# Attention, retention and gated-MLP blocks on one core: where head 0's values, modulation's loads and modulation's turning stand

## The chip, the cores and the metric

One core of one Trainium2 chip. The metric is the device time of one launch in microseconds, the median of the runs of a kernel. TensorE (PE) multiplies into PSUM, VectorE (DVE) and ScalarE (ACT) read PSUM and prepare operands, GpSimd (POOL) and SyncE (SP) issue the loads, POOL computes a few small powers too.

## The reference

Everything is float32 on 256 tokens of width 2048. The change touches the first layer, grouped-query attention with a gate, and the product that modulates the second block:

```python
proj = h @ w_in                                   # 2048 x 5120
q, k, v, g = jnp.split(proj, [...], axis=-1)      # 16 query heads, 4 key heads of 128
q = apply_rope(rms_norm(q, q_gain), cos, sin) * (A_HEAD_DIM ** -0.5)
k = apply_rope(rms_norm(k, k_gain), cos, sin)
s = jnp.einsum('bkgqd,bskd->bkgqs', qb, k)
p = jax.nn.softmax(s, axis=-1)
o = jnp.einsum('bkgqs,bskd->bkgqd', p, v)
return (o * jax.nn.silu(g)) @ w_out
...
x = layer_norm(ALPHA * x + y, ln_gain[i], ln_bias[i])
...
mod = silu(c) @ w_mod + b_mod                     # 2048 x 12288, for the second block
```

Behind it come a retention layer with eight heads, a second block of window and indexed attention, and a gated MLP.

## The kernel before

**Products in three passes.** A product of float32 matrices is made of three matmuls: rounded weights times rounded activations, weight rest times rounded activations, rounded weights times activation rest (`product`, L420 to L422). So each weight chunk is loaded (`raw`), rounded by ACT into `w_hi` (`round_hi`, L401) and its rest is made by VectorE into `w_lo` (`split_lo`, L406). Weights come in blocks of four chunks of 4 x 128 rows; SP loads a chunk of the next block, in two halves, when TensorE has finished the chunk that held the buffer (`load`, L366).

**Attention.** The four key heads are called heads 0 to 3 here, each with its four query heads. For head i TensorE runs `pe_attention`: a block for the queries (512 columns, block 4i - 1), a block for key and value (256 columns, block 4i), a block for the gate (512 columns, block 4i + 1) and, for i > 0, a block of the output projection of the head before (block 4i + 2). Head 0 has blocks 0 to 2. So head 1 has blocks 3, 4, 5 and 6, head 2 blocks 7 to 10. Between the gate's chunks stand the turning of the normed queries and keys (L559, `turn_qk`) and the scores (L659). Between the output's chunks stand, as `between(c)`, the turning of the probabilities (L669) and the values (L677). Head 0 has no output block: its `between` steps run back to back after its gate block, with 19 filler matmuls of `pe_fill` (L565) in them. Heads 1 to 3 are one hardware loop.

**Who waits for whom.** VectorE in `vec_attention` makes `w_lo` chunk by chunk, norms and rotates the queries (L1157 to L1168, with a power on POOL, L1586) and later the key, splits the turned head output into `a_oh` and `a_ol` (L1248), and multiplies the values by the gate into `a_og` (L1231). In between it adds up modulation's product, `mod_pair`, eight steps of 1 MB of `w_mod` per head (L1075, L1081). The sum of a head is turned by TensorE (`pe_mod`, L571) after chunk 1 of the next head's second block, and VectorE reads it (`mod_read`, L1090). The query turning waits for `a_ol` of the head before. After head 0 VectorE computes the retention layer's decay constants (`vec_decay`, L1424 to L1454, some 40 tiny operations), and ACT scales z by ALPHA (L1013).

**POOL's queue** is in order: for heads 1 to 3 two modulation loads (L1571), the power of the query norm, two loads, the power of the key norm, four loads. Each load waits until VectorE has used up the buffer.

```python
with g.Fori(1, A_KV) as i:
    loads(i, 0, 2)
    a_power(i, 0)
    loads(i, 2, 4)
    a_power(i, 1)
    loads(i, 4, 8)
```

## Time and profile before

| | |
|---|---|
| median of 3 runs | 2299.97 us (2297.93 to 2300.0) |
| the profiled execution, its own time | 2298.13 us |
| its span | 2296.4 us |
| TensorE busy | 2242.6 us, 98% of the span |
| VectorE busy | 1681.7 us, 73% |
| ScalarE busy | 994.6 us, 43% |
| mean granted clock of TensorE | 0.996 of full |

Busy time on TensorE is time with a matmul in flight. A timeline row gives the start and the time to the end of the last instruction in it, in us from the span's start; an entry in brackets is idle time of the engine ahead of the row and what ended it. The granted clock is a share of 2.4 GHz: 1.00 is that level, 0.50 the lower one of 1.2 GHz. The profiled execution's own time is 1.7 us above its span and 1.8 us below the median of the runs.

### The profile page before, as it was taken

The numbers are of one execution on the slowest core, as the hardware profiler recorded it, in microseconds if no ns is written. First come the engines' busy times: TensorE is split into PE (matmuls) and PEld (weight loads), VectorE is DVE, ScalarE is ACT, GpSimd is POOL, SyncE is SP. The second block draws the span as 40 slices with busy tenths as digits, with TensorE's granted clock in tenths as the row PEclk, the third lists the DMA queues.
The fourth block names the chain that finished last, engine by engine and source line by source line (L and its number), as shares of the span: only waits on it lengthen the run. The fifth ranks groups of instructions, "written<-read, shape, count | busy, mean of one in ns | idle before, by whom it ended". The sixth has DMA issues, their size and how long they took to land.

```text
span 2296.4 us, 28927 instructions
## 1 busy us (share of the span) xinstructions
PE 2242.6 (98%) x10724; PEld 1851.6 (81%) x10724; DVE 1681.7 (73%) x1871; ACT 994.6 (43%) x1017; POOL 141.6 (6%) x202
## 2 busy tenths in 40 slices
PE   7999999999999999999999999999999999999998
PEld 6888888888878888788787778777888888888886
DVE  5788877988877778677795676985655666665567
ACT  4543433534434434343443456454444344444434
POOL 2110010010000000000011001000000000000000
PEclk9999999999999999999999999999999999999999
DMA  7877775687777777777746546455555555555553
GB/s 256 287 262 258 262 257 202 203 327 274 269 263 274 261 255 274 257 269 270 244 167 202 187 138 166 145 166 183 184 184 194 188 183 189 192 186 183 192 190 131
DMA packets 260288, 503.57 MB, mean 219 GB/s; under 512 B 14705, under 2 KB 68385, under 8 KB 259328
## 3 DMA queue, kind: packets, MB, share of 16 engines
q1 hardware_dynamic: 228480, 381.73, 49.9%
q0 software_dynamic: 31376, 119.80, 15.1%
q10 hardware_dynamic: 368, 1.18, 0.1%
q8 instruction: 41, 0.67, 0.1%
q14 instruction: 23, 0.19, 0.0%
HBM read 498.90 MB, written 3.69 MB: 219 GB/s over the span
## 4 chain that ended last, share of the span: by engine, by line
PE 85%; DVE 6%; DMA 4%; issue 2%; ACT 2%; SPq 0%; POOL 0%; DVEq 0%; POOLq 0%; ACTq 0%
PE pair_t L420 26%; PE pair_t L422 25%; PE pair_t L421 25%; DMA raw<-in_attn_w_in_dram 2%; PE turn L559 2%; DVE w_lo L406 1%; ACT w_hi L401 1%; PE sc L827 1%; PE sc L819 1%; DVE m_acc L1081 1%; PE sc L1678 1%; PE sc L677 1%; PE sc L659 0%; PE turn L1687 0%; DMA raw<-in_w_down_dram 0%
## 5 line engine op out<-in xcount | busy, mean ns | idle before, releaser
L406 DVE TENSOR_TENSOR w_lo<-raw,w_hi 128x2048 fp32r<-128x2048 f32 (+1 forms) x364 | 815.8, 2243 | 486.6 <-ACT w_hi L401 482.2
L401 ACT ACTIVATE w_hi<-raw 128x2048 fp32r<-128x2048 f32 (+1 forms) x367 | 689.0, 1879 | 1037.5 <-DMA raw<-in_ret_w_in_dram 340.9
L420 PE MATMUL pair_t<-w_hi,x_hi 128*128 128x512 f32 (+1 forms) x2080 | 814.3, 392 | 15.1 <-DVE w_lo L406 9.2
L422 PE MATMUL pair_t<-w_hi,x_lo 128*128 128x512 f32 (+1 forms) x2080 | 799.4, 384 | 0.0
L421 PE MATMUL pair_t<-w_lo,x_hi 128*128 128x512 f32 (+1 forms) x2080 | 798.8, 384 | 0.0
L420 PEld LDWEIGHTS pair_t<-w_hi,x_hi 128*128 128x128 f32 x2080 | 393.1, 189 | 101.2 <-DVE w_lo L406 11.9
L422 PEld LDWEIGHTS pair_t<-w_hi,x_lo 128*128 128x128 f32 x2080 | 392.8, 189 | 78.0
L421 PEld LDWEIGHTS pair_t<-w_lo,x_hi 128*128 128x128 f32 x2080 | 393.4, 189 | 72.9 <-issue 0.2
L1081 DVE SCALAR_TENSOR_TENSOR m_acc<-m_raw,csilu,m_acc 128x1024 f32<-128x1024 f32 x180 | 230.8, 1282 | 7.0 <-DMA m_raw<-in_w_mod_dram 3.5
L420 PE MATMUL pair_t<-w_hi,f_hh 128*128 128x512 f32 x352 | 138.2, 393 | 1.8 <-DVE f_y L2261 0.8
L421 PE MATMUL pair_t<-w_lo,f_hh 128*128 128x512 f32 x352 | 137.0, 389 | 0.0
L422 PE MATMUL pair_t<-w_hi,f_hl 128*128 128x512 f32 x352 | 137.0, 389 | 0.0
L1571 POOL DMA_DIRECT2D m_raw<-in_w_mod_dram x96 | 68.9, 718 | 936.0 <-DVE m_acc L1081 921.3
L420 PE MATMUL pair_t<-w_hi,r_oh 128*128 128x512 f32 x256 | 102.8, 401 | 0.1
L422 PE MATMUL pair_t<-w_hi,r_ol 128*128 128x512 f32 x256 | 99.7, 390 | 0.0
L421 PE MATMUL pair_t<-w_lo,r_oh 128*128 128x512 f32 x256 | 99.6, 389 | 0.0
L420 PEld LDWEIGHTS pair_t<-w_hi,f_hh 128*128 128x128 f32 x352 | 66.1, 188 | 16.3 <-DVE f_y L2261 1.8
L422 PEld LDWEIGHTS pair_t<-w_hi,f_hl 128*128 128x128 f32 x352 | 66.1, 188 | 13.8
L421 PEld LDWEIGHTS pair_t<-w_lo,f_hh 128*128 128x128 f32 x352 | 66.1, 188 | 13.3
L1241 DVE TENSOR_TENSOR z<-z,pair_t 128x512 f32<-128x512 f32 x88 | 56.3, 681 | 14.5 <-PE pair_t L422 14.2
L2657 POOL TENSOR_TENSOR rstd<-var,minus_half 128x1 f32<-128x1 f32 x6 | 4.3, 711 | 870.9 <-DVE var L2250 870.9
L420 PEld LDWEIGHTS pair_t<-w_hi,r_oh 128*128 128x128 f32 x256 | 48.1, 188 | 12.0 <-issue 1.7
(362 smaller groups left out, 2145.1 us busy)
## 6 DMA issues: line engine op xcount, KB each, us to landing
m_raw<-in_w_mod_dram POOLq DMA_DIRECT2D x96, 1024.0 KB, 6.1
raw<-in_ret_w_in_dram SPq DMA_DIRECT2D x192, 512.0 KB, 4.6
raw<-in_w_up_dram SPq DMA_DIRECT2D x176, 512.0 KB, 4.2
raw<-in_w_down_dram SPq DMA_DIRECT2D x88, 512.0 KB, 4.6
raw<-in_attn_w_in_dram SPq DMA_DIRECT2D x64, 512.0 KB, 4.6
raw<-in_ret_w_out_dram SPq DMA_DIRECT2D x64, 512.0 KB, 4.8
raw<-in_w_in_dram SPq DMA_DIRECT2D x56, 512.0 KB, 4.5
raw<-in_attn_w_out_dram SPq DMA_DIRECT2D x32, 512.0 KB, 5.1
```

Source lines behind the costliest of these rows:

```text
L401: act.activation(chunk(w_hi, c, width), chunk(raw, c, width), ACT.Copy).then_inc(sem("hi"), 1)
L406: v.tensor_tensor(chunk(w_lo, c, width), chunk(raw, c, width), chunk(w_hi, c, width).bitcast(F32), ALU.subtract).then_inc(sem("lo"), 1)
L420: pe.matmul(to, xh, wh, start=start, stop=False)
L421: pe.matmul(to, xh, wl, start=False, stop=False)
L422: return pe.matmul(to, xl, wh, start=False, stop=stop)
L559: mm = pe.transpose(to[:, i * P:(i + 1) * P], src[:, t, m * P:(m + 1) * P], ident[:, :])
L677: mm = pe.matmul(sc[t][:, h * A_HD:(h + 1) * A_HD], a_pT[:, h % 2, k, t * P:(t + 1) * P], a_v[:, k, :], start=k == 0, stop=k == NT - 1)
L819: mm = pe.matmul(sc[0][:, s * T:(s + 1) * T], r_kT[:, k, s * P:(s + 1) * P], r_qT[:, k, :], start=k == 0, stop=k == 1)
L827: mm = pe.matmul(sc[t][:, :], r_s[:, s, t * P:(t + 1) * P], r_v[:, s, :], start=s == 0, stop=s == NT - 1)
L1081: ins = v.scalar_tensor_tensor(out=m_acc[:, :], in0=w, scalar=cc, in1=m_acc[:, :], op0=ALU.mult, op1=ALU.add)
L1241: ins = v.tensor_tensor(z[:, t, c * CB:(c + 1) * CB], z[:, t, c * CB:(c + 1) * CB], pair[order[c]][t][:, :], ALU.add)
L1571: g.dma_start(m_raw[:, u % 2, :, :], w_m[:, 2 * u:2 * u + 2, bass.ds(2 * step * CB, 2 * CB)])\
```

## The change

Head 1 is taken out of the hardware loop and written out; the loops run over heads 2 and 3. In it,

- TensorE's `between` steps of head 0 (turning the probabilities, values) stand after chunks 0, 1 and 2 of head 1's first block, and the fillers are gone;
- the turning of modulation's sum stands after chunk 3 of head 1's second block, not after chunk 1, and the turning of head 0's output `a_og` behind it, not before the block;
- VectorE splits that output (`vec_a_turn`) behind the key's norm, not behind the query's;
- chunk 3 of head 1's first block is rounded and split at the end of head 0, behind the last copy of turned probabilities;
- the decay constants are computed at the end of head 1, not of head 0, on VectorE and ACT;
- ACT scales the two halves of z between its roundings in head 1.

And for heads 1 to 3, POOL's first two modulation loads stand behind the query norm's power.

TensorE, the end of head 0 before, with the turnings of probabilities (a_p) and the values (a_v):

```order
L659 MATMUL sc<-a_kT,a_qT 128x256 x4
L669 MATMUL turn<-ident,a_p 128x128 x8
L565 MATMUL pair_t<-ident 128x128 x19
L677 MATMUL sc<-a_v,a_pT 128x128 x4
L669 MATMUL turn<-ident,a_p 128x128 x4
```

The same place in the changed kernel, followed by the end of head 1's second block (128x256), modulation's turning (m_acc) and the output's (a_og); "..." stands for the projection's matmuls:

```order
L660 MATMUL sc<-a_kT,a_qT 128x256 x4
L420 MATMUL pair_t<-w_hi,x_hi 128x512
...
L670 MATMUL turn<-ident,a_p 128x128 x8
...
L678 MATMUL sc<-a_v,a_pT 128x128 x4
...
L678 MATMUL sc<-a_v,a_pT 128x128 x8
...
L422 MATMUL pair_t<-w_hi,x_lo 128x256
L571 MATMUL sc<-ident,m_acc 128x128 x8
L559 MATMUL turn<-ident,a_og 128x128 x8
```

A wide chunk of head 1 now stands ahead of each piece of head 0, and both turnings stand behind the narrow block.

VectorE in head 1 of the changed kernel, from the query's last scaling to the split of the turned output (a_ol); before, the row of a_ol stood right behind the first `w_lo` row:

```order
L1186 TENSOR_TENSOR a_q<-a_q,a_rs 128x512 x2
L406 TENSOR_TENSOR w_lo<-raw,w_hi 128x4x256
L406 TENSOR_TENSOR w_lo<-raw,w_hi 128x2048
L1106 TENSOR_REDUCE modc<-sc 128x4 x2
...
L1186 TENSOR_TENSOR a_k<-a_k,a_rs 128x128 x2
L1270 TENSOR_TENSOR a_ol<-turn,a_oh 128x512 x2
```

The split of the output has moved from ahead of modulation's reading to behind the key.

POOL in the loop over the heads, before:

```order
L1571 DMA m_raw<-in_w_mod_dram 128x2x1024
...
L1581 REGISTER_ALU
L1586 TENSOR_TENSOR a_rs<-a_ss,minus_half 128x8
L1570 REGISTER_ALU
```

and in the changed kernel:

```order
L1626 ISA
L1610 TENSOR_TENSOR a_rs<-a_ss,minus_half 128x8
L1594 ISA
L1595 ISA
L1595 DMA m_raw<-in_w_mod_dram 128x2x1024
```

The power now comes first in each trip, and the loads that stood ahead of it follow it.

The diff:

```diff
@@ -608,6 +608,7 @@
 
         def pe_attention(pe, i):
             first = isinstance(i, int) and i == 0
+            second = isinstance(i, int) and i == 1
 
             def arrived(c):
                 if first:
@@ -617,23 +618,23 @@
                     pe.wait_ge(sem("a_sum_z"), 2 + 4 * (i - 1) - 1)
 
             def mod(c):
-                if c == 1 and not first:
+                if c == (3 if second else 1) and not first:
                     pe_mod(pe, i - 1)
 
             def turn_x(c):
                 if c < 2:
                     pe_turn_x(pe, c + 2)
-            project(pe, a_block(i, 0), pair[0], before=arrived, after=turn_x if first else None, lead=first)
-            if first:
-                pe_params(pe)
-            else:
-                pe_a_turn(pe, i)
+
+            def attend_first(c):
+                if c < 3:
+                    between(c + 1, 0)
 
             def kv_free(c):
                 if c == 0 and not first:
                     pe.wait_ge(sem("a_krot"), i)
                     pe.wait_ge(sem("a_sum_z"), 2 + 4 * (i - 1))
-            project(pe, a_block(i, 1), pair[1], width=2 * A_HD, before=kv_free, after=mod)
+                if c == 1 and second:
+                    pe.wait_ge(sem("a_og"), 1)
 
             def q_read(c):
                 if c == 0:
@@ -660,7 +661,7 @@
                                    a_kT[:, :], start=True, stop=True)
                 mm.then_inc(sem("a_score"), 1)
 
-            def turn_probs(h):
+            def turn_probs(h, i):
                 pe.wait_ge(sem("a_prob"), 4 * i + h + 1)
                 if h >= 2:
                     pe.wait_ge(sem(f"a_pT{h % 2}"), 2 * i + 1)
@@ -670,7 +671,7 @@
                                           a_p[:, h, t, k * P:(k + 1) * P], ident[:, :])
                 mm.then_inc(sem("a_p_turned"), 1)
 
-            def values(h):
+            def values(h, i):
                 pe.wait_ge(sem(f"a_pT{h % 2}"), 2 * i + h // 2 + 1)
                 for t in range(NT):
                     for k in range(NT):
@@ -691,27 +692,31 @@
                     scores(2)
                     scores(3)
 
-            def between(c):
+            def between(c, i=i):
 
                 if c == 1:
-                    turn_probs(0)
-                    turn_probs(1)
+                    turn_probs(0, i)
+                    turn_probs(1, i)
                 elif c == 2:
                     pe.wait_ge(sem("a_prob"), 4 * i + 4)
-                    values(0)
-                    turn_probs(2)
-                    values(1)
-                    turn_probs(3)
+                    values(0, i)
+                    turn_probs(2, i)
+                    values(1, i)
+                    turn_probs(3, i)
                 elif c == 3:
-                    values(2)
-                    values(3)
+                    values(2, i)
+                    values(3, i)
+            project(pe, a_block(i, 0), pair[0], before=arrived,
+                    after=turn_x if first else attend_first if second else None, lead=first)
+            if first:
+                pe_params(pe)
+            elif not second:
+                pe_a_turn(pe, i)
+            project(pe, a_block(i, 1), pair[1], width=2 * A_HD, before=kv_free, after=mod)
+            if second:
+                pe_a_turn(pe, i)
             project(pe, a_block(i, 2), pair[0], before=q_read, after=along_gate)
-            if first:
-                for c in range(CH):
-                    between(c)
-                    if c == 1:
-                        pe_fill(pe, pair[1][0], 19)
-            else:
+            if not first:
                 pe_a_output(pe, i, between)
 
         def pe_turn_x(pe, q):
@@ -839,7 +844,8 @@
             pe_turn_x(pe, 0)
             pe_turn_x(pe, 1)
             pe_attention(pe, 0)
-            with pe.Fori(1, A_KV) as i:
+            pe_attention(pe, 1)
+            with pe.Fori(2, A_KV) as i:
                 pe_attention(pe, i)
             pe_fill(pe, turn[0], 15)
             pe_a_turn(pe, A_KV)
@@ -857,8 +863,10 @@
         def act_attention(act, i, n, rest):
 
             first = isinstance(i, int) and i == 0
+            second = isinstance(i, int) and i == 1
             H = lambda j, c: round_hi(act, a_block(i, j), c, 2 * A_HD if j == 1 else CB)
-            H(0, 3)
+            if not second:
+                H(0, 3)
             for c in range(2 if first else 3):
                 H(1, c)
             act.wait_ge(sem("products"), CH * a_block(i, 0) + 4)
@@ -866,13 +874,19 @@
                 act.activation(a_sq[:, t, :], pair[0][t][:, :], ACT.Square).then_inc(sem("a_square"), 1)
             if first:
                 H(1, 2)
-            if not first:
+            if first:
+                act_params(act)
+            elif not second:
                 act_a_turn(act, i)
-            else:
-                act_params(act)
             H(1, 3)
+            if second:
+                act.wait_ge(sem("turned"), KC // 2)
+                act.wait_ge(sem("turn_lo"), KC // 2)
+                act.activation(z[:, 0, :], z[:, 0, :], ACT.Copy, scale=ALPHA).then_inc(sem("home"), 1)
             H(2, 0)
             H(2, 1)
+            if second:
+                act.activation(z[:, 1, :], z[:, 1, :], ACT.Copy, scale=ALPHA).then_inc(sem("home"), 1)
             H(2, 2)
             act.wait_ge(sem("products"), CH * a_block(i, 1) + 4)
             if not first:
@@ -882,6 +896,8 @@
             act.wait_ge(sem("a_qrot"), i + 1)
             for t in range(NT):
                 act.activation(a_sq[:, t, 0:A_HD], pair[1][t][:, 0:A_HD], ACT.Square).then_inc(sem("a_square"), 1)
+            if second:
+                act_a_turn(act, i)
             H(2, 3)
             act.wait_ge(sem("a_qk_turned"), 3 * i + 1)
             act.activation(a_qT[:, 0:2, :], gview(turn[0][:, :], 2), ACT.Copy).then_inc(sem("a_qT_act"), 1)
@@ -918,6 +934,8 @@
             if rest:
                 rest[1](1)
             turned(2)
+            if first:
+                round_hi(act, n, 3)
             if rest:
                 rest[1](2)
 
@@ -1006,16 +1024,14 @@
                 round_hi(act, 0, c)
             turn_hi(act, 0, True, range(6, 8))
             act_attention(act, 0, a_block(1, 0), None)
+
+            def rest_of(i):
+                return [lambda c: round_hi(act, a_block(i, 3), c), lambda c: round_hi(act, a_block(i + 1, 0), c)]
+            act_attention(act, 1, a_block(1, 3), rest_of(1))
             act_decay(act)
-            act.wait_ge(sem("turned"), KC // 2)
-            act.wait_ge(sem("turn_lo"), KC // 2)
-            for t in range(NT):
-                act.activation(z[:, t, :], z[:, t, :], ACT.Copy, scale=ALPHA).then_inc(sem("home"), 1)
             act.wait_ge(sem("toep"), 16)
-            with act.Fori(1, A_KV) as i:
-                act_attention(act, i, a_block(i, 3),
-                              [lambda c: round_hi(act, a_block(i, 3), c),
-                               lambda c: round_hi(act, a_block(i + 1, 0), c)])
+            with act.Fori(2, A_KV) as i:
+                act_attention(act, i, a_block(i, 3), rest_of(i))
             act_a_turn(act, A_KV)
             round_hi(act, R_B0 - 1, 3)
             round_hi(act, R_B0, 0)
@@ -1138,8 +1154,10 @@
 
             def M():
                 mod_pair(v, *todo.pop(0))
+            second = isinstance(i, int) and i == 1
             S_ = lambda j, c: split_lo(v, a_block(i, j), c, 2 * A_HD if j == 1 else CB)
-            S_(0, 3)
+            if not second:
+                S_(0, 3)
             for c in range(2 if first else 3):
                 S_(1, c)
                 if not first and c < 2:
@@ -1172,7 +1190,7 @@
                     if first:
                         vec_params(v)
                     S_(1, 3)
-                    if not first:
+                    if not first and not second:
                         vec_a_turn(v, i)
                     for c in range(3):
                         S_(2, c)
@@ -1183,6 +1201,8 @@
                             mod_read(v, i - 1)
                         if first or c < 2:
                             M()
+            if second:
+                vec_a_turn(v, i)
             S_(2, 3)
             if not first:
                 M()
@@ -1215,9 +1235,11 @@
                         rest[1](c - 1)
                 if c in (1, 2):
                     turned(2 * c - 1)
+                if first and c == 2:
+                    split_lo(v, n, 3)
                 if c < 3:
                     M()
-                elif first:
+                elif second:
                     vec_decay(v)
             assert not todo
             v.wait_ge(sem("a_prob"), 4 * i + 4)
@@ -1485,12 +1507,14 @@
                 split_lo(v, 0, c)
             turn_lo(v, 0, groups=range(6, 8))
             vec_attention(v, 0, a_block(1, 0), None)
-            with v.Fori(1, A_KV) as i:
-                vs.enter(i, 1, VEC_A)
-                vec_attention(v, i, a_block(i, 3),
-                              [lambda c: split_lo(v, a_block(i, 3), c),
-                               lambda c: split_lo(v, a_block(i + 1, 0), c)])
-            vs.leave(A_KV - 1)
+
+            def rest_a(i):
+                return [lambda c: split_lo(v, a_block(i, 3), c), lambda c: split_lo(v, a_block(i + 1, 0), c)]
+            vec_attention(v, 1, a_block(1, 3), rest_a(1))
+            with v.Fori(2, A_KV) as i:
+                vs.enter(i, 2, VEC_A)
+                vec_attention(v, i, a_block(i, 3), rest_a(i))
+            vs.leave(A_KV - 2)
             vec_layer_end(v, "a", R_B0 - 1, A_KV, 1)
             split_half(v, R_B0, 1, 0)
             turn_lo(v, 1, par[:, 0:KC], par[:, KC:2 * KC], behind={
@@ -1600,9 +1624,8 @@
             get(rows[:, 0, :], broadcast_row(ln_gain, 0, D), "rows_in")
             get(rows[:, 1, :], broadcast_row(ln_bias, 0, D), "rows_in")
             with g.Fori(1, A_KV) as i:
-                loads(i, 0, 2)
                 a_power(i, 0)
-                loads(i, 2, 4)
+                loads(i, 0, 4)
                 a_power(i, 1)
                 loads(i, 4, 8)
```

## Rows read from the trace of the kernel before

**Rows 1.** The page, part 1: busy us, share of the span, instructions.

```profile
PE 2242.6 (98%) x10724; PEld 1851.6 (81%) x10724; DVE 1681.7 (73%) x1871; ACT 994.6 (43%) x1017; POOL 141.6 (6%) x202
```

**Rows 2.** PE timeline, head 0 into 1: start, us, instruction, [idle before <-releaser].

```profile
84.54 1.04 PE L669 MATMUL turn<-ident,a_p 128*128 128x128 f32 x8
85.42 4.41 PE L565 MATMUL pair_t<-ident 128*128 128x128 f32 x38
95.86 0.47 PE L420 MATMUL pair_t<-w_hi,x_hi 128*128 128x512 f32 x1
...
117.75 1.03 PE L559 MATMUL turn<-ident,a_og 128*128 128x128 f32 x8
```

**Rows 3.** DVE timeline, 106 to 149 (head 0's end and head 1).

```profile
106.89 2.16 DVE L1231 SCALAR_TENSOR_TENSOR a_og<-sc,a_rinv,a_sg 128x128 f32<-128x128 f32 x8
...
112.90 1.22 DVE L406 TENSOR_TENSOR w_lo<-raw,w_hi 128x1024 fp32r<-128x1024 f32 x1 [1.65 <-ACT w_hi L401]
...
120.21 1.22 DVE L406 TENSOR_TENSOR w_lo<-raw,w_hi 128x1024 fp32r<-128x1024 f32 x1
...
128.26 1.22 DVE L406 TENSOR_TENSOR w_lo<-raw,w_hi 128x1024 fp32r<-128x1024 f32 x1
129.40 1.28 DVE L1248 TENSOR_TENSOR a_ol<-turn,a_oh 128x512 fp32r<-128x512 f32 x2
...
135.01 1.28 DVE L1090 TENSOR_REDUCE modc<-sc 128x512 f32 x2
...
147.96 0.49 DVE L1168 TENSOR_TENSOR a_k<-a_k,a_rs 128x128 f32<-128x128 f32 x2
```

**Rows 4.** PE timeline, waits and query turnings (L559).

```profile
51.58 0.58 PE L420 MATMUL pair_t<-w_hi,x_hi 128*128 128x256 f32 x1 [4.29 <-DVE w_lo L406]
...
135.15 0.80 PE L420 MATMUL pair_t<-w_hi,x_hi 128*128 128x512 f32 x1 [2.48 <-DVE w_lo L406]
...
147.77 1.03 PE L559 MATMUL turn<-ident,a_q 128*128 128x128 f32 x8
...
226.54 0.50 PE L420 MATMUL pair_t<-w_hi,x_hi 128*128 128x512 f32 x1 [0.29 <-DVE w_lo L406]
...
237.85 1.04 PE L559 MATMUL turn<-ident,a_q 128*128 128x128 f32 x8
```

**Rows 5.** Busy us (x count) of PE, PEld, DVE, ACT, POOL; PEclk; DMA share; GB/s.

```profile
50.00:56.00 6.00, 4.42 (x20) 4.42 (x21) 5.09 (x4) 5.67 (x4) 0.00 (x0) 0.50 0.32 119
99.40:106.70 7.30, 7.30 (x34) 6.05 (x33) 6.20 (x39) 7.02 (x5) 1.81 (x3) 1.00 0.75 270
118.54:124.38 5.84, 5.84 (x51) 5.84 (x50) 5.74 (x10) 1.61 (x5) 2.19 (x2) 1.00 0.98 326
195.00:214.00 19.00, 19.00 (x93) 15.95 (x92) 9.93 (x8) 4.53 (x5) 1.43 (x2) 1.00 0.58 178
```

**Rows 6.** PE timeline, head 1's output block, values and turnings after chunk 2.

```profile
180.66 1.05 PE L677 MATMUL sc<-a_v,a_pT 128*128 128x128 f32 x8
...
183.24 0.48 PE L420 MATMUL pair_t<-w_hi,a_oh 128*128 128x512 f32 x1
```

**Rows 7.** Head 2: SP and POOL timelines, and us to landing of those two halves.

```profile
216.43 0.93 SPq L366 DMA_DIRECT2D raw<-in_attn_w_in_dram  x2
...
216.49 1.65 POOL L1586 TENSOR_TENSOR a_rs<-a_ss,minus_half 128x8 f32<-128x8 f32 x1 [4.80 <-DVE a_ss L1159]
...
DMA to landing us min/median/max: 4.5/4.9/5.2
```

**Rows 8.** The same in a retention head: halves behind a POOL load.

```profile
855.68 0.71 POOL L1571 DMA_DIRECT2D m_raw<-in_w_mod_dram  x1 [11.55 <-DVE m_acc L1081]
...
856.16 0.93 SPq L366 DMA_DIRECT2D raw<-in_ret_w_in_dram  x2
...
DMA to landing us min/median/max: 6.3/6.7/7.1
```

**Rows 9.** Landing of block 5's chunk 0 in head 1, behind POOL's load.

```profile
DMA to landing us min/median/max: 7.0/7.7/8.4
```

## Prediction

> **What bounds the kernel now.** I read the page's busy shares first: TensorE is busy for 98% of the span [rows 1], so a change pays only where it takes out one of the few stretches in which TensorE waits, fills or runs at a low clock. The second view is TensorE's timeline where the change cuts. Between the last scores of head 0 (84.54) and the first projection of head 1 (95.86) stand 11.32 us, of which 4.41 are filler matmuls [rows 2]; head 1's first block then takes 21.89 us for four chunks, 5.5 each, and ends at 117.75. The third is VectorE's timeline behind it [rows 3]: from 106.89 to 148.38 VectorE works nearly without a break, and what TensorE needs in head 1 comes out of that one sequence. The fourth are TensorE's waits on it [rows 4], with the granted clock and the busy time of four stretches [rows 5] and one piece of head 1 that prices the moved code [rows 6]. The last is how loads of the SP and POOL queues land when both are asked for at once [rows 7 to 9].
>
> **Head 0's values between head 1's chunks.** Chunk 0 of block 3 (head 1's first) can start when the scores and the gate's reader are done, at about 84.6; its split copies are ready, and that of chunk 3 is now made inside head 0. The work put between the chunks is 0.88 us for the first turning (84.54 to 85.42), 2.58 (180.66 to 183.24, the same code in head 1's output block) and for the last two values at most 2.0, since two such and two turnings make the 2.58 [rows 2, 6]: 5.4 us. Block 3 ends at 84.6 + 21.9 + 5.4 = 111.9 in place of 117.75, 5.9 earlier; the fillers and the waits around them are gone.
>
> **Does VectorE follow?** Its decay constants (99.4 to 106.7, [rows 5]) move out of the way. The head's output a_og now waits for the last values, one chunk before 111.9, so 106.4: it starts at 106.5 and takes 2.1. Chunk 0's split of block 4 to chunk 2's start is 120.21 - 112.90 = 7.3, so chunk 2 begins at 115.9; from there to the end of chunk 3's split are 129.48 - 120.21 = 9.3 us of square sums, rotation and scaling of the queries [rows 3], which ends at 125.2. TensorE, whose turnings now stand behind the block, runs three narrow chunks (two took 5.84, [rows 5]) in 8.8 us and is ready for chunk 3 at 120.7. **A new wait of 4.5 us** stands there. A wait of 4.29 us in head 0 was followed by a granted clock of 0.50 [rows 4, 5], the 1.2 GHz level: 20 narrow matmuls took 4.42 us, so 24 take 5.2 to 5.3 and not 2.9 to 3.0: 2.3 more. Block 4 ends at 130.5, modulation's turning 0.8 later at 131.3.
>
> VectorE then waits for that turning before it reads it (before, it stood behind chunk 1 and nobody waited). From the read (135.01) to the end of a_k (148.38) are 13.4 us, and the split of the turned output, 1.2 net, now comes behind a_k [rows 3]. So the query turning, which asks for that split, starts at 131.3 + 13.4 + 1.2 = 145.9; it was 147.77 [rows 4]. Only 1.9 us of the 5.9 are left. TensorE has been idle since 143.2 (131.3, 0.8 for the head's turning, two chunks), 2.7 us. Behind the wait of 2.48 at 135.15 the same two chunks took 12.6 us to the query turning, in head 2 11.3 [rows 4]: 1.3 us for the clock, and I charge that once more. **Head 1 gives 0.6 us.** Bounds: 4.2 if no clock is lost (1.9 + 2.3), and a loss of about 1 if the low clock lasts longer in both places.
>
> **Decay constants at head 1's end** cost nothing: VectorE is busy for 9.93 of the 19 us between 195 and 214 [rows 5], so 9.1 idle us cover 7.2. Without the cover the next a_og would be late for the turning at the end of the block. The scaling of z in ACT goes into ACT's waits for loads (ACT is busy for 4.53 of those 19 us, 1.61 of the 5.84 after 118.54, [rows 5]). Chunk 3's rounding and split in head 0 were due anyway and only come earlier. PE's extra code is unrolled; the trace shows no time for that.
>
> **Modulation's loads behind the query norm's power.** In head 1 they went ahead of the raw chunks of block 5 and held them (7.0 and 8.4 us to land, [rows 9]); there the change helps, but that wait was replaced above. In heads 2 and 3 it does something else. The power starts at 216.49 and takes 1.65 [rows 7]; its input comes 1.7 us earlier when no POOL load stands before chunk 2, so it ends at 216.5, and both 1 MB loads go out there. SP issues the two halves of block 9's chunk 0 (the gate projection of head 2) at 216.43 and 0.56 later, and they landed in 4.5 and 5.2 us with nothing beside them [rows 7]. A half issued 0.48 us behind a POOL load took 6.3 us, the next one 7.1 [rows 8]. In the changed kernel the second half is about 0.45 behind, so it lands at 217.0 + 6.3 = 223.3 and not 222.2. ACT and VectorE round and split it at once, TensorE already waits 0.29 us for it at 226.54 [rows 4], and VectorE's sequence up to a_k starts from it. **Heads 2 and 3 lose 1.1 us each.** Bounds: +0.7 gained (the half keeps its 4.5) to 3.2 lost (it takes 8.4, as in [rows 9]).
>
> The trace lets the queue that came first go first: the pair in [rows 9] waited for nearly the whole POOL load. The Trainium skill, "DMA: Bandwidth & Descriptors", section "Queues, rings and completion order", says that each DMA engine alternates between the queues at packet granularity. By that rule the 1 MB chunk and the 1 MB load would share from the start, the chunk would be 1 to 2 us late, and the worst bound could not occur; [rows 9] disagree, so I keep it.
>
> **Sum.** -0.6 + 2 x 1.1 = +1.6 us on the profiled execution's own time of 2298.13, so 2299.7. That execution lies 1.8 us below the median of the runs, 2299.97; on the median's scale the forecast is **2301.6 us**. About 0.2% (4.6 us) is what a measurement of this kernel can tell from no change, so I call this the same.
>
> **Rivals.**
> Faster: TensorE's clock stays up through both waits of head 1 (4.2 us) and the POOL loads come behind both raw halves, which land in 4.5 us (0.7 each): -5.6, 2294.4. For it: POOL's and SP's issues lie within 0.1 us of each other by my sum, and the landings in [rows 7] were free of any load. Against: the 4.29 and 2.48 us waits both did. It decides at a wait in head 1 below about 2 us. Chance 0.17.
> Slower: in heads 2 and 3 POOL's two loads get ahead of the whole chunk 0. Its second half lands like the 8.4 of [rows 9], 3.2 us late, and the wait of then some 3.5 us costs the clock (1.3): 4.5 x 2 - 0.6 = +8.4, 2308.4. It decides as soon as POOL issues before SP's first half at 216.43. For it: the two are even by my sum. Against: the power needs TensorE's last chunk, and SP needs only one chunk more. Chance 0.18.
> The loads' move does nothing in heads 2 and 3 because POOL issues behind both halves: -0.6, 2299.4. Chance 0.20.
> The forecast: 0.42. Something not named: 0.03.
>
> **Numbers.** Faster by over 0.2% is the first rival, 0.17. Slower by over 0.2% is the second with the upper edge of the forecast, 0.22. The same is 0.61. The range takes in the forecast and the third rival with their bounds and about half of each outer rival: 2295.0 to 2307.0.
>
> **What would show it.** Right: no fillers, block 3 done near 112; VectorE's chunk 3 of block 4 near 125 with TensorE waiting 4 to 5 us and a lowered granted clock; the query turning of head 1 near 146 behind a_ol; in heads 2 and 3 a wait of 1 to 2 us for chunk 0 of the third block. Wrong: a head 1 that keeps most of 5.9 us, or heads 2 and 3 that are no longer than before, or over 3 us longer each.

## The result and the profile after

The changed kernel took 2306.13 us in the median of eight runs (2303.46 to 2316.54), the kernel before, measured beside it, 2299.98 (2297.93 to 2304.02): ratio 1.0036, 95% interval [1.0021, 1.005] (the two medians alone give 1.0027). It is slower by 6 us; the forecast was +1.6 and no change that can be measured. Measured again later, with eleven runs, it gave 2303.42 and a ratio of 1.0023 [1.0009, 1.0038], 4.1 us above the median beside it. The profiled execution took 2303.46, 5.3 us more than that of before.

TensorE's share is a point lower, its idle time is up. Page, part 1:

```profile
span 2301.8 us, 28756 instructions
PE 2239.5 (97%) x10686; PEld 1849.7 (80%) x10686; DVE 1682.0 (73%) x1871; ACT 992.9 (43%) x1016; POOL 141.5 (6%) x202
```

TensorE's timeline where head 0's values now stand between head 1's chunks, and through head 1 (start, us, instruction, [idle before <-releaser]); it answers [rows 2, 4]:

```profile
84.95 0.50 PE L420 MATMUL pair_t<-w_hi,x_hi 128*128 128x512 f32 x1 [0.18 <-ACT a_sg L920]
...
119.87 0.38 PE L420 MATMUL pair_t<-w_hi,x_hi 128*128 128x256 f32 x1 [1.71 <-DVE w_lo L406]
...
127.83 0.58 PE L420 MATMUL pair_t<-w_hi,x_hi 128*128 128x256 f32 x1 [4.83 <-DVE w_lo L406]
...
132.24 1.04 PE L571 MATMUL sc<-ident,m_acc 128*128 128x128 f32 x8
133.11 1.04 PE L559 MATMUL turn<-ident,a_og 128*128 128x128 f32 x8
...
147.78 1.65 PE L559 MATMUL turn<-ident,a_q 128*128 128x128 f32 x8 [2.73 <-DVE a_ol L1270]
...
213.89 1.03 PE L559 MATMUL turn<-ident,a_og 128*128 128x128 f32 x8
...
235.95 0.50 PE L420 MATMUL pair_t<-w_hi,x_hi 128*128 128x512 f32 x1 [2.80 <-DVE w_lo L406]
...
307.55 1.03 PE L559 MATMUL turn<-ident,a_og 128*128 128x128 f32 x8
...
323.88 0.50 PE L420 MATMUL pair_t<-w_hi,x_hi 128*128 128x512 f32 x1 [2.92 <-DVE w_lo L406]
```

The fillers are gone and head 1's first projection starts at 84.95 in place of 95.86. The query turning of head 1 still starts at 147.78, where it was 147.77. Two waits before the chunks of block 4 and one before the query turning have eaten all of it. Two more waits of 2.80 and 2.92 us in heads 2 and 3 were 0.29 in head 2 before [rows 4].

VectorE over the same stretch (answers [rows 3]):

```profile
118.59 1.23 DVE L406 TENSOR_TENSOR w_lo<-raw,w_hi 128x1024 fp32r<-128x1024 f32 x1 [2.09 <-ACT w_hi L401]
...
126.55 3.42 DVE L406 TENSOR_TENSOR w_lo<-raw,w_hi 128x1024 fp32r<-128x1024 f32 x2
133.31 1.29 DVE L1106 TENSOR_REDUCE modc<-sc 128x4 f32<-128x512 f32 x2 [3.34 <-PE sc L571]
...
146.44 1.28 DVE L1270 TENSOR_TENSOR a_ol<-turn,a_oh 128x512 fp32r<-128x512 f32 x2
```

The split of chunk 2 waits for its rounded copy, and so for the second raw half; the norm and chunk 3's split come behind it, and then VectorE itself waits 3.34 us for TensorE's turning of modulation's sum. The granted clock in block 4's last chunk and behind the query turning, and VectorE in head 1's output block (answers [rows 5]: busy us of PE, PEld, DVE, ACT, POOL; clock; DMA share; GB/s):

```profile
127.70:132.20 4.50, 4.37 (x24) 4.37 (x25) 2.27 (x2) 1.70 (x1) 0.00 (x0) 0.62 1.03 418
147.80:156.20 8.40, 8.40 (x35) 7.19 (x36) 7.74 (x6) 2.40 (x2) 0.73 (x1) 0.80 0.60 197
195.00:214.00 19.00, 19.00 (x86) 15.67 (x85) 16.95 (x48) 5.13 (x5) 0.00 (x0) 1.00 0.43 140
```

VectorE takes the decay constants (16.95 us busy for 9.93) without a wait of TensorE behind them.

**Where the raw halves were.** SP and POOL timelines in head 1, and the landing of each of SP's two halves of block 4's chunk 2 (256 KB each; the POOL loads are 1 MB each):

```profile
105.35 1.33 SPq L366 DMA_DIRECT2D raw<-in_attn_w_in_dram  x2
105.97 0.71 POOL L1595 DMA_DIRECT2D m_raw<-in_w_mod_dram  x1 [10.12 <-DVE m_acc L1097]
106.68 0.57 POOL L1566 DMA_DIRECT2D rows<-in_ln_gain_dram  x1
107.24 0.54 POOL L1566 DMA_DIRECT2D rows<-in_ln_bias_dram  x1
...
DMA to landing us min/median/max: 3.1/3.1/3.1
...
DMA to landing us min/median/max: 11.2/11.2/11.2
```

The first half, issued at 105.4, landed in 3.1 us. The second was issued at 106.3, 0.3 us behind POOL's load of `w_mod`, and took 11.2. The chain of work that leads to the query turning (view `--critical`) runs through this half:

```profile
106.30 11.18 DMA raw<-in_attn_w_in_dram
```

In head 2 the same happens with block 9's chunks (the halves of chunk 0, issued before POOL, in the first landing row; those of chunk 1, issued behind it, in the second):

```profile
217.97 3.81 SPq L366 DMA_DIRECT2D raw<-in_attn_w_in_dram  x4
218.97 1.46 POOL L1595 DMA_DIRECT2D m_raw<-in_w_mod_dram  x2
...
DMA to landing us min/median/max: 3.7/4.2/4.6
...
DMA to landing us min/median/max: 9.4/9.8/10.2
```

In head 3 POOL's first load went out at 311.70, 0.07 us behind SP's first half and ahead of its second, which took 7.4 us; there TensorE waits for chunk 0. In the second trace of the change POOL's load in head 3 went out 0.06 us ahead of SP's first half; the second half took 8.3 us:

```profile
308.13 1.46 POOL L1595 DMA_DIRECT2D m_raw<-in_w_mod_dram  x2
308.19 0.93 SPq L366 DMA_DIRECT2D raw<-in_attn_w_in_dram  x2
...
321.33 0.79 PE L420 MATMUL pair_t<-w_hi,x_hi 128*128 128x512 f32 x1 [3.81 <-DVE w_lo L406]
```

### The profile page after: what moved, and what is told of

Its sections match the earlier page's. It is cut to its first block, busy times and chain, and to the rows that moved or that the text cites. A ratio compares the mean times of both kernels' runs of the same rounds, so it can differ in the third digit from the quotient of the medians.

```text
span 2301.8 us, 28756 instructions
## 1 busy us (share of the span) xinstructions
PE 2239.5 (97%) x10686; PEld 1849.7 (80%) x10686; DVE 1682.0 (73%) x1871; ACT 992.9 (43%) x1016; POOL 141.5 (6%) x202
## 4 chain that ended last, share of the span: by engine, by line
PE 85%; DVE 6%; DMA 5%; issue 2%; ACT 2%; SPq 0%; POOL 0%; DVEq 0%; POOLq 0%; ACTq 0%
PE pair_t L420 26%; PE pair_t L422 25%; PE pair_t L421 25%; DMA raw<-in_attn_w_in_dram 2%; PE turn L559 2%; DVE w_lo L406 1%; ACT w_hi L401 1%; PE sc L832 1%; PE sc L824 1%; DMA raw<-in_ret_w_in_dram 1%; PE sc L678 1%; PE sc L1701 1%; PE sc L660 0%; PE turn L1710 0%; PE sc L559 0%
```

## The experiments

The table sets all traces against each other. Head 1 is counted from the end of head 0's last scores (before: 82.82 + 1.89 = 84.71) to the output turning behind head 1 (212.35), heads 2 and 3 from there to the next such turning (303.73, 377.81). The column "from its 1st" counts head 1 from its first projection, where that stands right behind the scores; it leaves out a wait for ACT that differs between executions (part 2). The medians come from 5 to 12 runs each, beside 8 to 35 runs of the kernel before on the same chip (medians 2299.2 to 2300.0). Two values stand where a kernel was measured twice.

```
kernel                                       head 1        from its 1st  head 2       head 3       median us        ratio to before
before                                       127.6         -             91.4         74.1         2300.0           1
the change                                   129.1 127.9   128.9 128.2   93.7 94.4    76.1 77.0    2306.1 2303.4    1.0036 1.0023
before, loads moved in all heads             125.4         -             92.4         76.4         2302.6           1.0019
before, loads moved in head 1 only           125.6         -             91.4         73.8         2297.3           0.9991
change, loads back in all heads              128.8 128.3   129.2 128.7   92.1 92.9    73.8 73.9    2299.0 2302.3    1.0000 1.0012
the same, POOL's head 1 written out          133.1         131.0         92.1         73.8         2302.3           1.0004
change, 72 fillers in the wait for chunk 3   128.0         128.3         95.8         77.3         2310.7           1.0044
change, loads moved in head 1 only           130.6 128.1   129.0 128.5   91.8 92.4    73.8 73.7    2303.5 2302.5    1.0020 1.0016
 + rows' loads late                          127.2 125.7   126.5 126.0   92.7 91.6    73.7 73.7    2297.5 2298.1    0.9996 0.9995
 + 36 fillers in the wait for chunk 3        126.0 125.0   126.3 125.4   93.1 92.8    73.7 73.8    2301.6 2301.0    1.0013 1.0008
rows late + split of chunk 3 early           124.6         125.0         92.1         74.5         2297.4           0.9989
  + output split early                       122.9 121.1   121.3 121.4   91.7 92.1    74.0 74.1    2292.3 2293.1    0.9966 0.9977
  the same, loads ahead of power in head 1   126.8         124.8         91.9         73.9         2296.6           0.9985
  the same, rows' loads early                126.4         124.7         91.6         73.6         2297.0           0.9988
```

A trace is one execution, and not always a typical one. In the 20 traces head 0's last scores end between 79.99 and 85.21 us, a spread of 5.2 us ahead of everything that the edits touch. The heads are therefore compared by their own lengths.

**1. POOL's order, put back in the changed kernel and made alone in the kernel before.**

```diff
# loads back: in the changed kernel
             with g.Fori(1, A_KV) as i:
+                loads(i, 0, 2)
                 a_power(i, 0)
-                loads(i, 0, 4)
+                loads(i, 2, 4)
# loads only: the reverse of this, in the kernel before
```

> The change with POOL's queue as it was before (two of modulation's loads ahead of the query norm's power in heads 1 to 3). Theory A (in heads 2 and 3 the moved loads hold chunk 1 of the third block, and that costs what the changed profile shows there, 2.3 and 2.0 us with the low clock): heads 2 and 3 are 91.4 us long again from output turning to output turning (93.7 in head 2 of the changed kernel), the time is 4 us below the changed kernel, about 2302. Rival B (the written-out head 1 and its new order of work cost the time, POOL's order does not matter): heads 2 and 3 keep their waits of 2.8 and 2.9 us, the time stays at 2306.

> The kernel before with POOL's part alone (power first, then four loads, in heads 1 to 3). Theory A: heads 2 and 3 lose about 2 us each to a wait for chunk 1 of the third block; head 1 loses its wait of 2.48 us for block 5's chunk 0 and the 1.3 us of low clock behind it, or gets a new one for chunk 1 as in heads 2 and 3: 2300 + 4.3 and up to 3.8 less, 2300.5 to 2304.3. Rival B: 2300, nothing moves.

> The change with power-first in head 1 alone; heads 2 and 3 have their two loads ahead of the power again. Theory A: head 1 as in the changed kernel (output turning of head 1 at 213.9, 1.5 us later than before), heads 2 and 3 91.4 us each: 2301.5. Rival B: 2306. Against e1 this tells whether the loads' place matters in head 1 at all: if it does by the wait for block 5's chunk 0, e1 is 1 to 2 us slower than this one.

> The kernel before, with modulation's loads behind the query norm's power in head 1 alone (POOL's head 1 written out, heads 2 and 3 as before). In the run that moved the loads in all heads of the kernel before, head 1 (output turning at 208.0, scores of head 0 done at 82.65) was 125.4 us long and not 127.6, and heads 2 and 3 together 3.3 longer. Theory: the order costs in heads 2 and 3 alone, so this kernel keeps the 2.2 us of head 1: 2297. Rival: writing POOL's head 1 out is what made the run with power first in head 1 (2303.45) slower than the one with all loads back (2299.0): then this one is 3 to 4 us slower than before, 2303, though its head 1 is shorter.

Put back, the change is at 2299.0, ratio 1.0 [0.999, 1.0009], where the theory had 2302; made alone, the move gives 2302.57, 1.0019 [1.0007, 1.0031]. Head 2 of the changed kernel with the loads back, and head 3 of the kernel before with the loads moved:

```profile
227.82 0.50 PE L420 MATMUL pair_t<-w_hi,x_hi 128*128 128x512 f32 x1 [1.49 <-DVE w_lo L406]
```

```profile
317.06 0.50 PE L420 MATMUL pair_t<-w_hi,x_hi 128*128 128x512 f32 x1 [3.24 <-DVE w_lo L406]
```

Read from the table, the move costs in heads 2 and 3 together 169.8 - 165.9 = 3.9 us in the changed kernel (the second pair: 171.3 - 166.8 = 4.5) and 168.8 - 165.2 = 3.6 in the kernel before. In head 1 of the kernel before it gains 2.1: alone there it gives 2297.28, 0.9991 [0.9981, 1.0002], as its theory had it; by the median that gain is within the interval. So the move has two signs: a gain where it frees block 5, a loss in the heads where it meets block 9. The medians of the changed kernel with and without it lie 7.1 us apart in the first measurements and 1.2 in the second ones, which were made on one chip and whose intervals overlap; the traces, 4.2 and 4.1 over the three heads, lie between. So the size rests on the traces.

Head 2 of the kernel before with the loads moved is the case that the forecast had priced: POOL's load went out at 212.32, 0.22 us behind SP's first half, the second half took 5.9 us and the head is 1.0 us longer, for a forecast of 1.1; TensorE's wait there is 1.44 us.

**2. The two measured again, and POOL's head 1 written out.** The kernels with and without power first in head 1 differed by 4.4 us at the same profiled span, 2299.4. POOL's loop was run from head 2, and head 1's calls stood ahead of it, in the old order.

> The changed kernel with POOL's old order in all heads, as the run with all loads back (2299.0), but with POOL's head 1 written out, as in the run with power first in head 1 alone (2303.45). Those two had the same profiled span, 2299.4, and medians 4.4 us apart. Theory: power first in head 1 is what costs, through the clock or the loads of block 5, and this kernel is at 2299. Rival: writing POOL's head 1 out costs by itself (its place in memory or its timing), and this kernel is at 2303.

> The same kernel as the one with power first in head 1 alone, again. Theory: its time of 2303.45 holds, within 1.5 us. Rival: the run before it drew late instances of a kernel whose waits stand near a tie, and it comes out at 2299 to 2301.

> The changed kernel itself, on one chip with its variants. Theory: its 2306.1 holds within 1.5 us, with waits of 2.8 to 5 us for block 9's chunks 0 or 1 in heads 2 and 3, whichever of the two queues issued first. Rival: a part of its 6 us was the chip or the draw, and it is at 2302 to 2303 here.

> The changed kernel with POOL's old order in all heads, again. Theory: 2299.0 holds within 1.5 us, so that POOL's order is worth 5.5 to 7 us of the changed kernel's time. Rival: it comes out like its two relatives with POOL's head 1 written out (2302.3 to 2303.5), and the order is worth 3 to 4 us, what the traces of heads 2 and 3 show.

Written out it gave 2302.27, 1.0004 [0.9993, 1.0014]; power first in head 1 again 2302.52, 1.0016 [1.0006, 1.0025]; the loads back again 2302.27, 1.0012 [1.0001, 1.0023]; the change again 2303.42, so its 2306.1 did not hold within 1.5 us either. So the 2299.0 was not repeated, and neither the order in head 1 nor the writing out shows a cost in this kernel: the two that differ only in that order, measured on one chip, have medians of 2302.27 and 2302.52. The trace of the written-out one shows one thing that differs between executions:

```profile
85.28 0.50 PE L420 MATMUL pair_t<-w_hi,x_hi 128*128 128x512 f32 x1 [2.18 <-ACT a_sg L920]
```

With the fillers gone, the first projection of head 1 stands right behind ACT's reading of the gate; that wait was 0.18 in the profiled run of the change and between none and 2.18 in the others. It makes up 2.2 of the 133.1 us in the table. In the change itself the two traces make head 1 1.5 and 0.2 us longer than the one trace of the kernel before, so what is shown is that head 1 gained nothing, and not that it lost 1.5.

**3. The layer norm's rows.** In the kernel before, POOL issued the two 1 MB loads of them at 100.55 and 101.11. They held block 4's chunk 0, whose halves took 9.2 and 9.5 us, and TensorE did not wait for them: it needed that chunk at 118.54. Chunk 2's halves went out 11.5 us later and landed in 3.0 and 3.4. In the changed kernel chunk 2's halves go out 7.3 us earlier, at 105.35 and 106.30, and POOL's loads 6 us later, at 106.68, because the `w_mod` load ahead of them waits for VectorE until 105.97. So they meet chunk 2.

```diff
-            get(rows[:, 0, :], broadcast_row(ln_gain, 0, D), "rows_in")
-            get(rows[:, 1, :], broadcast_row(ln_bias, 0, D), "rows_in")
             a_power(1, 0)
             loads(1, 0, 4)
             a_power(1, 1)
             loads(1, 4, 8)
+            get(rows[:, 0, :], broadcast_row(ln_gain, 0, D), "rows_in")
+            get(rows[:, 1, :], broadcast_row(ln_bias, 0, D), "rows_in")
             with g.Fori(2, A_KV) as i:
```

> As e3, and the two 1 MB loads of the norm's rows, which POOL issued at the end of head 0, stand at the end of head 1. Theory A': in the changed kernel the second half of block 4's chunk 2 landed at 117.5, 11.2 us after its issue, behind modulation's load and these two; that made TensorE wait 1.7 us for chunk 2 and moved VectorE's sequence by 2 to 2.7 us. Without them it lands near 113, VectorE's chunk 2 starts at 116 and the query turning of head 1 comes at 145.5 and not 147.8: 2 us below e3, 2299.5. Rival: VectorE was not held by that chunk, or the moved loads hold something in head 1's output block: same as e3, 2301.5, or more.

> The version with power first in head 1 alone and the rows' loads late, again, beside the one with fillers on one chip. Theory: 2297.46 was a lucky draw by up to 2 us, since the three traces of heads 1 to 3 give it 0.5 us more than the kernel before: 2299 to 2300. Rival: 2297.5 holds.

2297.46, 0.9996 [0.9983, 1.0009], where the theory had 2299.5, and again 2298.12, 0.9995 [0.9983, 1.0007]. With one POOL load beside it and not three, the second half of chunk 2 landed in 7.2 us:

```profile
105.82 1.33 SPq L366 DMA_DIRECT2D raw<-in_attn_w_in_dram  x2
106.43 0.71 POOL L1595 DMA_DIRECT2D m_raw<-in_w_mod_dram  x1 [10.10 <-DVE m_acc L1097]
...
DMA to landing us min/median/max: 2.9/5.1/7.2
```

And its TensorE timeline:

```profile
126.11 0.58 PE L420 MATMUL pair_t<-w_hi,x_hi 128*128 128x256 f32 x1 [4.61 <-DVE w_lo L406]
...
145.89 1.83 PE L559 MATMUL turn<-ident,a_q 128*128 128x128 f32 x8 [2.72 <-DVE a_ol L1270]
```

TensorE no longer waits for chunk 2, and the query turning starts at 145.89: what the forecast had for the change itself. Counted from its first projection, head 1 is 2.5 and 2.4 us shorter than with the rows early. The medians are 6.0 us apart where both were measured on one chip, and 4.4 in the second, on two chips; the part above 2.5 no trace shows.

**4. The clock.** What the waits of head 1 were followed by, in all traces with a wait of about 2.7 to 3.0 us at the query turning. Chunk 3 has 24 matmuls, which take 2.9 us behind no wait.

```
trace                               wait before   chunk 3    granted clock, 6.6 us   query turning to
                                    chunk 3, us   took, us   from query turning on   output turning, us
the change                          4.83          4.41       0.74                    66.1
  second                            4.82          4.24       0.74                    66.1
loads back in all heads             3.40          5.29       1.00                    64.5
  second                            3.42          5.29       1.00                    64.4
the same, POOL's head 1 written out 5.12          5.09       0.74                    66.0
loads moved in head 1 only          3.33          4.22       0.74                    66.1
  second                            4.81          5.28       1.00                    64.5
 + rows' loads late                 4.61          4.25       0.74                    66.1
  second                            4.61          5.29       1.00                    64.5
 + 36 fillers                       0.59          2.96       0.74                    67.1
  second                            0.58          2.97       0.74                    66.1
change, 72 fillers                  none          2.96       1.00                    64.4
rows late + split of chunk 3 early  none          2.89       0.74                    66.1
```

In the nine traces without fillers or early split the wait before chunk 3 was followed by a granted clock of 0.50 to 0.66 over the chunk. In four of them the chunk took 5.3 us, which the forecast had, and the clock behind the next wait was 1.00; in four it took 4.2 to 4.4 and the clock behind the next wait was lowered too; one had 5.1 and the lowered clock behind the next wait. Two of the kernels that were traced twice show one execution of either kind.

Fillers on TensorE in the wait for block 4's chunk 3: first 72, twice the intended number (8.20 us), in the changed kernel, then 36 in the kernel of part 3.

```diff
                 if c == 1 and second:
                     pe.wait_ge(sem("a_og"), 1)
+                if c == 3 and second:
+                    pe_fill(pe, turn[0], 18)
```

> The changed kernel with 36 filler matmuls (the form of which 38 took 4.41 us) on TensorE in its wait for chunk 3 of block 4 in head 1. Theory: the wait of 4.83 us is what lowers the clock; with the fillers the 24 matmuls of chunk 3 take 3.0 us and not 4.4 to 5.3, modulation's turning comes 1.5 to 2 us earlier (130.5), VectorE's wait of 3.34 for it shrinks as much, the query turning starts at 146 and the kernel gains 1.5 to 2 us on the changed kernel's 2306.1: 2304.3. Rival: the clock follows something else, nothing moves by over 0.5 us, and there may even be a later loss, because the fillers end behind the split.

> The version with power first in head 1 alone and the rows' loads late (2297.46; its chunk 3 of block 4 waited 4.61 us and took 4.41 us at a low clock), with 36 fillers of 0.114 us, 4.1 us, in that wait. Theory: the wait lowers the clock; without it chunk 3 takes 3.0 us and modulation's turning, which VectorE waits for, comes 1.4 us earlier, and the query turning too (144.5 in place of 145.9): 2296.1. Rival: the granted clock falls all the same or at the next wait (2.72 us at the query turning), and the kernel is where it was, 2297.5.

> The same with 36 fillers in the wait for chunk 3 of block 4. Its trace had head 1 1.2 us shorter (125.99 against 127.17), its median was 4.1 us longer, in another job. Theory: the trace is right, and beside its twin on one chip it is 1 us faster (2298 to 2299). Rival: the fillers cost in most runs, for instance because they end behind the split or the clock falls at the next wait more often: 2 us or more slower than its twin, 2301.

TensorE's timeline in the second profiled run of the version with 36:

```profile
118.27 4.18 PE L565 MATMUL turn<-ident 128*128 128x128 f32 x36
...
123.03 0.38 PE L420 MATMUL pair_t<-w_hi,x_hi 128*128 128x256 f32 x1 [0.58 <-DVE w_lo L406]
```

Its windows for the chunk behind the fillers and the one behind the query turning, and then the same two of its twin without fillers:

```profile
123.00:126.20 3.20, 3.17 (x26) 3.17 (x27) 2.18 (x1) 2.23 (x2) 0.00 (x0) 1.00 1.03 410
143.40:150.00 6.60, 6.60 (x27) 5.45 (x26) 5.89 (x6) 1.55 (x1) 0.73 (x1) 0.87 0.43 139
```

```profile
126.10:130.60 4.50, 4.49 (x27) 4.49 (x28) 2.15 (x1) 1.92 (x2) 0.00 (x0) 0.68 1.04 417
147.70:154.40 6.70, 6.70 (x29) 5.54 (x28) 5.94 (x6) 1.60 (x1) 0.73 (x1) 0.87 0.50 165
```

The fillers keep the clock at 1.00, the 2.4 GHz level, in the chunk behind them, whose 24 matmuls take 3.0 us and not 4.3. But behind the next wait, 2.72 us for a_ol, it is lowered in both traces with 36 fillers (the windows shown start 1.8 us into the turning; from its start on they have 0.74). In the twin without them it is lowered in the first trace, shown above, and not in the second:

```profile
141.40:148.00 6.60, 6.60 (x34) 5.66 (x35) 6.56 (x6) 2.41 (x2) 0.73 (x1) 1.00 0.51 160
```

Head 1, from its first projection, is 0.2 and 0.7 us shorter in the traces; the medians are 2301.56 and 2300.96 against 2297.46 and 2298.12 of the twin, 4.1 us longer on two chips and 2.8 on one, where the intervals overlap. The theories' 2296.1 and 2298 to 2299 did not come; in the second measurement the rival's 2301 did. Where that comes from no trace shows: heads 1 to 3 of both profiled runs are near those of the twin. It stays open. The version with 72 fillers (`pe_fill(pe, turn[0], 36)`) gave 2310.65, for a forecast of 2304.3, 1.0044 [1.0032, 1.0056]; its fillers ended 3.0 us later than TensorE could have started chunk 3, and its trace has the worst case of POOL's order in head 2: POOL issued 0.06 us **ahead** of SP's first half.

```profile
215.99 1.46 POOL L1597 DMA_DIRECT2D m_raw<-in_w_mod_dram  x2
216.05 0.93 SPq L366 DMA_DIRECT2D raw<-in_attn_w_in_dram  x2
...
DMA to landing us min/median/max: 3.7/6.6/9.5
```

```profile
230.43 0.80 PE L420 MATMUL pair_t<-w_hi,x_hi 128*128 128x512 f32 x1 [5.05 <-DVE w_lo L406]
```

Chunk 0's second half took 9.5 us, TensorE waited 5.05, and heads 2 and 3 took 173.1 us, 165.5 before and 169.8 and 171.3 in the change.

**5. VectorE's order.** On the kernel of part 3.

```diff
# split early, in vec_attention
+            if second:
+                S_(1, 3)
             for kind in range(2):
...
-                    S_(1, 3)
+                    if not second:
+                        S_(1, 3)
# output split early, on top of it
                         S_(2, c)
+                        if c == 0 and second:
+                            vec_a_turn(v, i)
...
-            if second:
-                vec_a_turn(v, i)
             S_(2, 3)
# and act_a_turn likewise between H(2, 0) and H(2, 1)
```

> The version with power first in head 1 alone and the rows' loads late (2297.46), and VectorE splits chunk 3 of block 4 ahead of the query norm of head 1. Theory: the 5.9 us of the filled gap were lost because VectorE's norm stood ahead of the split that TensorE waits for, and VectorE then waited 3.3 us for modulation's turning. With the split ahead TensorE's wait of 4.61 us at 126.1 is below 1 us, block 4 ends near 124.5, VectorE doesn't wait for the turning, and the query turning starts at 143 in place of 145.9: 2.9 us less, 2294.6. Rival: VectorE's sequence is as long in any order, TensorE's wait only moves to the query turning (5 us and more), and the gain is below 0.5 us: 2297.

> The kernel with the early split, and the split of head 0's turned output ahead of the key's norm: VectorE does it behind chunk 0 of block 5 and not behind a_k. Theory: the query turning waits for the split because the turned output stands in the same PSUM tile; without it in the way the query turning starts behind a_q, about 1.5 us earlier than in the kernel with the early split, of which 1 us stays (a_k is the next wait): 2293.6. Rival: a_k is what ends the wait, and VectorE now waits for TensorE's turning of the output: no gain or a loss of up to 1 us against the kernel with the early split.

> The version with both splits ahead, again: 2292.3 was the median of five runs. Theory: it stays 6 to 8 us ahead of the kernel before, 2292 to 2294. Rival: its relatives with the loads first (2296.6) and the rows early (2297.0) are what it is really like, and it comes out at 2296.

With chunk 3's split alone: 2297.35, 0.9989 [0.9977, 1.0001]. TensorE no longer waits in block 4, but in block 5 and longer at the query turning:

```profile
126.42 0.47 PE L420 MATMUL pair_t<-w_hi,x_hi 128*128 128x512 f32 x1 [2.45 <-DVE w_lo L406]
133.36 0.50 PE L420 MATMUL pair_t<-w_hi,x_hi 128*128 128x512 f32 x1 [1.23 <-DVE w_lo L406]
...
142.09 1.94 PE L559 MATMUL turn<-ident,a_q 128*128 128x128 f32 x8 [2.98 <-DVE a_ol L1273]
```

Its waits of 4.61 and 2.72 us became 2.45, 1.23 and 2.98: 7.3 us before, 6.7 now. The theory had 2294.6, the rival 2297: the rival's number came, though head 1 is 1.0 to 1.6 us shorter in the trace. With the output split moved too: 2292.3, 0.9966 [0.9953, 0.9979], and again 2293.13, 0.9977 [0.9965, 0.999].

```profile
140.93 1.03 PE L559 MATMUL turn<-ident,a_q 128*128 128x128 f32 x8
142.89 0.33 PE L559 MATMUL sc<-ident,a_k 128*128 128x128 f32 x1 [0.92 <-DVE a_k L1188]
```

The query turning waits for nothing; 0.92 us for a_k is left, and the clock holds: the turning takes 1.03 us where it took 1.94. I had given this step 1 us; counted from its first projection, head 1 shrank by 3.7 and 3.6. It is faster than both kernels: by 7.2 and 6.2 us than before, and by 10.3 than the change where the two were measured side by side.

**6. The best version with the other orders.** Loads ahead of the power in head 1, and the rows early again.

```diff
# loads first
+            loads(1, 0, 2)
             a_power(1, 0)
-            loads(1, 0, 4)
+            loads(1, 2, 4)
# rows early: the two get(rows...) ahead of a_power(1, 0)
```

> The version with both splits ahead (2292.3), with the loads ahead of the power in head 1 too, so that POOL's order is the old one in every head. Theory: in head 1 the order is worth little now, because VectorE and not a raw chunk sets block 5: 2292 to 2293. Rival: modulation's loads issued at 112 to 116 hold the chunks of block 5 as they did in the kernel before (7.0 to 8.4 us to land), and TensorE's two waits of 2.26 and 1.36 us grow by 1 to 2 us together: 2294.

> The version with both splits ahead (2292.3), with the two 1 MB loads of the layer norm's rows ahead of head 1's power again, where the changed kernel has them. Theory: they hold the second half of chunk 2 of block 4, which landed after 11.2 us in the changed kernel and after 7.2 where the rows came late; VectorE's early split of chunk 3 stands behind that, TensorE waits some 2 us for chunk 2 and the kernel is 2 to 3 us slower: 2294.8. Rival: with both splits ahead VectorE's slack in head 1 hides it: below 0.5 us.

2296.61, 0.9985 [0.9975, 0.9995], and 2297.03, 0.9988 [0.9979, 0.9997]: each costs some 4 us by the medians, which come from different chips, and 3.3 to 3.6 by head 1 from its first projection. The forecasts (2292 to 2293 with 2294 as the rival, and 2294.8) were too low for both. Here the first projection waits 4.49 us, below, for chunk 0 of block 5, and 4.22 with the rows early (2.26 in the best version).

```profile
132.95 0.77 PE L420 MATMUL pair_t<-w_hi,x_hi 128*128 128x512 f32 x1 [4.49 <-DVE w_lo L406]
```

So once VectorE's order is right, the raw chunks do cost head 1, and the change's own order of POOL is the right one there.

## Why the prediction was wrong

- **Block 3 ends at 111.9, fillers gone**: right (112.25 by the last projection). Decay constants free: right.
- **"Chunk 2 begins at 115.9"**: wrong, the first step that failed. I took 7.3 us from the kernel before, where chunk 2's raw halves were there in time. Block 4 came 5.9 us earlier, and I didn't ask what POOL's queue did at that time: a load of `w_mod` and the rows' two, 3 MB, held the second half for 11.2 us. Chunk 2's split ended at 119.8, TensorE waited 1.71. Experiment 3 takes the rows' loads away: VectorE goes from chunk 0's split to chunk 2's in 7.30 us again, and TensorE starts chunk 3 of block 4 40.7 us behind head 1's first projection in both traces, my 125.2 - 84.6 = 40.6. That the query turning then came at 145.89, my 145.9, is in part luck: that execution started its first projection 0.8 us later than I had it and ran chunk 3 1.1 us faster. Counted from the first projection the turning comes at 60.5 and 61.5, forecast 61.3, and in the change at 62.8 and 62.1.
- **A wait of 4.5 us before chunk 3**: 4.83, at 127.83 and not 125.2. The clock charge was too large there (the chunk took 4.4 us, not 5.2 to 5.3) and right behind the query turning: from it to the output turning 66.11 us, before 64.58, so 1.5 for my 1.3. The table of part 4 has four traces with the forecast's 5.3 and nothing lost behind the query turning. I charged the sum of both, 3.6 us; in eight of the nine traces with both waits unfilled it was 2.3 to 3.1.
- **Query turning at 145.9, "head 1 gives 0.6 us"**: 147.78, and head 1 is 129.11 - 127.64 = 1.5 us longer. Of the 1.9 at the turning, 2.6 are chunk 3's late start (0.35 of it because block 3 ended that much later than forecast), less 0.9 for the faster chunk 3; from the end of block 4 to VectorE's reading of modulation's sum were 1.07 us and not 0.8, and the rest of VectorE's sequence took 14.5 for my 14.6. The second trace has head 1 0.2 us longer. In either, the 0.6 did not come.
- **"Heads 2 and 3 lose 1.1 us each"**: wrong in size, 2.3 and 2.0 in the trace (3.0 and 2.9 in the second). I let one half of chunk 0 come 1.1 us late. In head 2 the power started 0.7 us earlier in the head than before (217.35 - 213.89 against 216.49 - 212.35), and not 1.7, so POOL issued 1.00 us behind SP; chunk 0 was free (4.6 us) and both halves of chunk 1 took 9.4 and 10.2: the next pair in SP's queue, which I hadn't followed. In head 3 it was chunk 0's second half, 7.4 us for my 6.3.
- **Sum**: the profiled execution is 5.3 us longer, forecast 1.6. Head 1 accounts for 2.1 of the difference, heads 2 and 3 for 2.1; the rest of the program gave 0.4 back. Over both traces, heads 2 and 3 are the larger miss: 4.3 and 5.9 us for 2.2.
- **The slower rival** (2308.4) had the right resource and the right kind of price. Its condition, POOL ahead of SP's first half, came true twice, each time by 0.06 us: in head 3 of the change's second trace (8.3 us for the second half and a wait of 3.81; the rival had 8.4 and 3.5) and with 72 fillers (9.5 and 5.05). The first of these heads is 2.9 us longer than before, not 4.5; the change pays nearly as much without the condition, because halves that SP issues 0.3 us and more behind POOL's load are held. The faster rival fell: the clock dropped at the waits, and the landings were not free. The third, POOL behind both halves, had its condition in head 2 of both traces (1.00 and 0.95 us behind the first half) and not its price: the next pair of halves was held instead.
- **Packets.** The Trainium skill, "DMA: Bandwidth & Descriptors", section "Queues, rings and completion order", says that each DMA engine alternates between the queues by the packet. I took that for an even share of the bytes, which would make a chunk 1 to 2 us late, and set [rows 9] against it. The trace agrees with the Trainium skill and not with my even share. While chunk 2's second half was held, from 110.5 to 114.5 us, the two queues moved (packets as the profile counts them, MB, share of the 16 DMA engines; q0 is POOL's, q1 SP's):

```profile
q0 software_dynamic: 269, 1.56, 94.7%
q1 hardware_dynamic: 196, 0.10, 8.5%
```

  The numbers of packets are near each other, but a packet of POOL's had 5.8 KB and one of SP's 0.5 KB. So SP's queue got a sixteenth of the bytes, and the half took 11.2 us where the one ahead of POOL's loads took 3.1. In head 2, from 225 to 229 us, it was 275 packets with 1.07 MB and 236 with 0.48: SP's wide halves have packets of 2.0 KB there. The bound of [rows 9] was right to keep, but it did not contradict the Trainium skill.

## What to carry to other kernels

When an edit lets a stage start earlier, look up what every other DMA queue issues at the new time, and follow the transfers behind the first one. Removing a filled gap on the bounding engine pays only if the engine that feeds it is put in a new order too: here the gap alone gave nothing, and two moved splits on VectorE, on top of the better order of the loads, gave 5 us. Where two queues issue within a few tenths of a microsecond of each other, one profile shows one side of it: the same half took 5.9 us with POOL 0.22 us behind SP's first half, 7.4 to 7.7 at 0.02 to 0.11 behind and 8.3 and 9.5 at 0.06 ahead.
